# Hybrid attention/DeltaNet block on one core: half of two blocks' output projection in the lead, inverse sums spread behind a unit's products, no threshold search around block ends

## The chip, the cores and the metric

One NeuronCore of a Trainium2 chip runs the whole program. The metric is the device time of one execution in microseconds (us).

## The reference

One encoder layer over 2048 tokens of width 1024, in float32:

```python
h = rms_norm(x, norm_mix_g);  proj = h @ w_in
o_a = sparse_indexer_attention(...)   # 8 heads of 64, top 256 keys of an indexer's score
o_b = gated_deltanet(...)             # 4 heads of 128, chunks of 64
x = x + concatenate([o_a, o_b]) @ w_out
h = rms_norm(x, norm_ffn_g)
x = x + square(relu(h @ w_ff1)) @ w_ff2      # width 4096
return rms_norm(x, norm_final_g)
```

What matters here is the line with `w_out`. Its 1024 input rows are 512 rows of attention output and 512 rows of DeltaNet output. The DeltaNet half of all tokens is known before attention starts.

## The kernel before

The program has three phases. The first normalises and projects, the second runs the DeltaNet, the indexer's scores and the rest of the projection, and the third (`attention_and_mlp`) runs attention, the output projection and the MLP. Only the third is touched.

**Blocks, tiles, units.** The third phase treats 16 tiles of 128 tokens in 4 blocks of 512. Attention is done in 64 units `u` (two heads of a tile, four units a tile). A unit is: scores (L2210, L2211) into PSUM, mask and maximum on VectorE (L2040, L2047), exponential on ScalarE (L1932), transposes (L2225), a high part on ScalarE (L1921) and a low part on VectorE (L2060), products with the values (L2243), the lower half copied on ScalarE (`low`, L1927), and `finish` on VectorE (L2020, L2024), which multiplies by the inverse sums. The inverse sums (reciprocal, L2067) are spread over the partitions by two small transposes, `spread` (L2252). Queries and keys are rotated and split beforehand by `prep` items, three for each tile (`sin` L1799, `add` L1806 and `prep_low` L1812 on GpSimd, `cos` L2073 on VectorE).

**Dense work.** Every float32 product is three fp32r matmuls (`three`, L2140 to L2142: high by high, high by low, low by high). For each block the dense stream is O (output projection, 8 chains of 24 matmuls), then W1 and W2. Weights come in units of 128x1024, are loaded by SyncE (`weights`, L1694), rounded on ScalarE (L1905) and have their low part made on GpSimd (`split`, L1784). A block uses 72 units, 288 in all. A dense step is half a unit: 12 matmuls of 512 columns. Its input, the mix, is split into `ah` and `al` by `mix_high` (ScalarE, L1898) and `mix_low` (VectorE, L2013), eight pieces a block: four are loaded (`mix_in`, L1760) from the DeltaNet's result through two buffers, four are the attention's rows. `x_add` (L1962) adds a chain of O to the residual; squares, their sum (L1969, PE L2191), `root`, `norm` (L1993) and `h_high` (L1888) follow.

**Threshold search.** For tiles 8 to 15 the 256th largest score is found bit by bit: `probe` on ScalarE (L1841 counts over up to 2048 columns, L1843 and L1847 set the bit), 31 probes a tile, and 11 `select` steps on VectorE (begin, turn, fix and so on). That makes 8 times 42 = 336 steps, one behind another.

**Order.** `OverlapPlan` writes all this into numbered slots. In each slot every engine's steps stand in the order of `ORDER`, and every engine runs its own list strictly in order, with semaphore waits. Slots below 0 are the lead: block 0's attention (units 0 to 15, three slots each, `LEAD` 58 slots before slot 0) with no dense work. From slot 0 a block has 147 slots: 144 dense steps and 3 without, while the next block's units are spread over it (`begins`). Search steps run from slot 2 to 377. `weights` for unit n stands one slot behind the split of unit n-2, and the splits of weight units 0 and 1 stand five slots behind the first. `search`, `mlp` and `attention` of the plan fill the lists; `number` counts banks.

```python
if i == 0:
    self.put("pe", end, "spread", u)      # ORDER has spread before product
self.put("pe", end, "product", u, i)
...
s = self.unit_slot[n - 2] if n >= 2 else self.first + 5
self.put("pool", s, "split", n)
...
if u: pe.wait_ge(norm_done, u)            # in spread: the bank shared with product is free
pe.wait_ge(rinv_done, u + 1)
```

## Time and profile before

| | |
|---|---|
| median of 3 runs | 3702.31 us (3700.27 to 3706.99) |
| profiled execution | 3707.24 us, span 3705.4 us, mean granted TensorE clock 0.959 |
| third phase | from about 1414 us; first dense step at 1539.3 us |
| busy | PE 3309.7 (89%), PEld 2733.7 (74%), DVE 2159.5 (58%), ACT 2160.7 (58%), POOL 1347.2 (36%) |
| chain that ended last | PE 28%, ACT 16%, DVE 9%, issue 5%, POOL 2%, DMA 1% |
| DMA | 395.42 MB, mean 107 GB/s |

The span is what the hardware profiler saw from the first to the last instruction. PE is the matmul, PEld the weight load beside it. The granted clock of TensorE is given as a share of 2.4 GHz, so 0.5 is 1.2 GHz. Since matmuls are pipelined, a PE that is shown busy all the time may still run below its full pace; the number of matmuls in a stretch and PEld tell that.

### The profile page before, as it was taken

What the parts mean: (1) busy time and instruction counts of PE and PEld (TensorE: products, weight loads), DVE (VectorE), ACT (ScalarE), POOL (GpSimd) and SP (SyncE); (2) the same over time, 40 slices, a digit from 0 to 9 for tenths busy, and PEclk for the clock granted to TensorE, in tenths of its full rate; (3) what the DMA queues carried; (4) which work ended last, traced back from release to release, by engine and by line L of the source; (5) the groups of instructions that cost most, each with busy time, mean ns of one, the idle gap of its engine ahead of it and who ended that gap; (6) DMA issues with size and microseconds to landing.
All of it is one profiled execution on the core that took longest, in us unless ns stands there. A gap on an engine that the chain in (4) does not pass through costs nothing.

```text
span 3705.4 us, 47047 instructions
## 1 busy us (share of the span) xinstructions
PE 3309.7 (89%) x16674; PEld 2733.7 (74%) x16674; DVE 2159.5 (58%) x3704; ACT 2160.7 (58%) x3717; POOL 1347.2 (36%) x713
## 2 busy tenths in 40 slices
PE   6999878888899995789899889999889999989998
PEld 4888757777777773668787668788668878868886
DVE  6344038687977764646646675748676575443223
ACT  4222138577755653587696869696868944433232
POOL 0211053434345444334444333433323333334443
PEclk9999989999999996899999999999999999999999
DMA  3512253423433444323333433334333333332222
GB/s 118 238 57 85 88 122 74 126 65 74 118 97 80 102 130 117 105 77 125 109 103 119 135 105 104 113 107 129 117 110 119 102 110 97 97 128 91 97 97 80
DMA packets 282664, 395.42 MB, mean 107 GB/s; under 512 B 22832, under 2 KB 204208, under 8 KB 277808
## 3 DMA queue, kind: packets, MB, share of 16 engines
q1 hardware_dynamic: 277680, 360.97, 32.0%
q10 hardware_dynamic: 4752, 31.46, 2.3%
q8 instruction: 134, 2.20, 0.2%
q14 instruction: 98, 0.80, 0.1%
HBM read 320.61 MB, written 71.73 MB: 106 GB/s over the span
## 4 chain that ended last, share of the span: by engine, by line
PE 28%; ACT 16%; DVE 9%; issue 5%; POOL 2%; DMA 1%; SPq 0%; ACTq 0%; DVEq 0%; POOLq 0%
PE m_ps L2140 7%; PE m_ps L2142 7%; PE m_ps L2141 7%; ACT m_junk L1841 6%; ACT m_wh L1905 2%; PE m_ps L2243 2%; POOL m_wl L1784 2%; PE m_ps L2225 2%; ACT m_prob L1932 1%; ACT m_verdict L1843 1%; ACT m_trial L1847 1%; ACT m_phi L1921 1%; PE m_ps L2210 1%; PE m_ps L2211 1%; DVE m_rl L1980 1%
## 5 line engine op out<-in xcount | busy, mean ns | idle before, releaser
L1784 POOL TENSOR_TENSOR m_wl<-m_raw,m_wh 128x1024 fp32r<-128x1024 f32 x288 | 719.0, 2497 | 1327.6 <-ACT m_wh L1905 1327.6
L2140 PE MATMUL m_ps<-m_ah,m_wh 128*128 128x512 f32 x1280 | 523.4, 409 | 25.1 <-DVE m_al L1997 17.3
L2142 PE MATMUL m_ps<-m_ah,m_wl 128*128 128x512 f32 x1280 | 507.0, 396 | 0.0
L2141 PE MATMUL m_ps<-m_al,m_wh 128*128 128x512 f32 x1280 | 505.8, 395 | 0.0
L2140 PE MATMUL m_ps<-m_th,m_wh 128*128 128x512 f32 x1024 | 414.9, 405 | 17.9 <-DVE m_tl L1982 11.3
L2142 PE MATMUL m_ps<-m_th,m_wl 128*128 128x512 f32 x1024 | 404.5, 395 | 0.0
L1841 ACT ACTIVATE m_junk<-m_sc,m_trial 128x1152 int8<-128x1152 f32 (+7 forms) x248 | 401.5, 1619 | 4.4 <-DVE m_sc L2100 3.3
L2141 PE MATMUL m_ps<-m_tl,m_wh 128*128 128x512 f32 x1024 | 403.6, 394 | 0.0
L1905 ACT ACTIVATE m_wh<-m_raw 128x1024 fp32r<-128x1024 f32 x288 | 302.9, 1052 | 146.8 <-PE m_ps L2142 138.9
L1980 DVE TENSOR_TENSOR m_rl<-m_rl 128x512 f32<-128x512 f32 x128 | 104.5, 816 | 358.5 <-ACT m_th L1861 358.1
L2140 PEld LDWEIGHTS m_ps<-m_ah,m_wh 128*128 128x128 f32 x1280 | 244.7, 191 | 79.9 <-DVE m_al L1997 20.1
L1921 ACT ACTIVATE m_phi<-m_ps 128x512 fp32r<-128x512 f32 (+1 forms) x288 | 164.2, 571 | 227.7 <-PE m_ps L2225 223.3
L2060 DVE TENSOR_TENSOR m_plo<-m_ps,m_phi 128x512 fp32r<-128x512 f32 (+1 forms) x288 | 189.4, 658 | 176.2 <-ACT m_phi L1921 174.9
L1975 DVE TENSOR_TENSOR m_acc<-m_acc,m_ps 128x512 f32<-128x512 f32 x256 | 175.0, 684 | 190.5 <-PE m_ps L2142 188.7
L2142 PEld LDWEIGHTS m_ps<-m_ah,m_wl 128*128 128x128 f32 x1280 | 244.0, 191 | 53.5
L1228 DVE SCALAR_TENSOR_TENSOR i_score<-i_relu,i_w,i_score 128x512 f32<-128x512 f32 (+3 forms) x266 | 255.1, 966 | 48.0 <-ACT i_relu L1086 33.6
L2141 PEld LDWEIGHTS m_ps<-m_al,m_wh 128*128 128x128 f32 x1280 | 245.1, 191 | 44.2 <-issue 0.5
L1086 ACT ACTIVATE i_relu<-i_ps 128x512 f32<-128x512 f32 (+3 forms) x304 | 156.0, 546 | 171.8 <-PE i_ps L884 135.0
L2140 PEld LDWEIGHTS m_ps<-m_th,m_wh 128*128 128x128 f32 x1024 | 195.1, 191 | 58.2 <-DVE m_tl L1982 13.0
L2142 PEld LDWEIGHTS m_ps<-m_th,m_wl 128*128 128x128 f32 x1024 | 194.6, 190 | 42.6
L2040 DVE CUSTOM_DVE_ANT_0 m_prob<-m_ps,m_bias 128x512 f32<-128x512 f32 (+3 forms) x320 | 192.2, 606 | 57.2 <-PE m_ps L2211 55.7
L2141 PEld LDWEIGHTS m_ps<-m_tl,m_wh 128*128 128x128 f32 x1024 | 195.4, 191 | 36.1
(324 smaller groups left out, 7470.3 us busy)
## 6 DMA issues: line engine op xcount, KB each, us to landing
m_raw<-w_units SPq DMA_DIRECT2D x288, 512.0 KB, 3.3
m_vals<-valsT SPq DMA_DIRECT2D x240, 128.0 KB, 3.4
p_raw<-w_proj SPq DMA_DIRECT2D x72, 256.0 KB, 4.1
m_rot<-rowsQ SPq DMA_DIRECT2D x50, 256.0 KB, 4.4
projT<-work ACTq DMA_DIRECT2D x12, 1024.0 KB, 4.5
g_qkvz<-projT SPq DMA_DIRECT2D x16, 768.0 KB, 5.5
wraw<-w_proj SPq DMA_DIRECT2D x21, 512.0 KB, 5.0
i_rot<-projT SPq DMA_DIRECT2D x32, 256.0 KB, 5.0
```

The lines of the kernel that those rows point to most:

```text
L1086: nc.scalar.activation(relu[:, c % RELUS, 0:w], ips[:, c % 2, 0:w], ACT.Relu).then_inc(relu_done, 1)
L1228: nc.vector.scalar_tensor_tensor(out=to, in0=relu[:, c % RELUS, 0:w], scalar=w_idx[:, j, h:h + 1], in1=to, op0=ALU.mult, op1=ALU.add).then ...
L1784: nc.gpsimd.tensor_tensor(wl[:, n % 3, :], raw[:, n % 2, :], wh[:, n % 3, :].bitcast(fp32), ALU.subtract).then_inc(w_lo, 1)
L1841: turns.do(nc.scalar.activation(junk[:, 0:N], sc[:, 0:N], ACT.Sign, scale=-1.0, bias=trial[:, :].bitcast(fp32), accum_out=balance[:, :]))
L1905: nc.scalar.activation(wh[:, n % 3, :], raw[:, n % 2, :], ACT.Copy).then_inc(w_hi, 1)
L1921: nc.scalar.activation(p_hi[:, m % 2, 0:w], t_bank(r)[:, 0:w], ACT.Copy).then_inc(hi_done, 1)
L1975: nc.vector.tensor_tensor(acc[:, k, :], acc[:, k, :], f_bank("W2", b, g, k), ALU.add).then_inc(y_added, 1)
L2040: nc.vector.tensor_tensor_reduce(out=prob[:, u % 2, h, 512 * p:512 * p + w], in0=s_bank(n)[:, 0:w], in1=bias[:, 512 * p:512 * p + w], scal ...
L2060: nc.vector.tensor_tensor(p_lo[:, m % 2, 0:w], t_bank(r)[:, 0:w], p_hi[:, m % 2, 0:w].bitcast(fp32), ALU.subtract).then_inc(lo_done, 1)
L2140: nc.tensor.matmul(dst, hi, rh, start=first, stop=False)
L2141: nc.tensor.matmul(dst, hi, r_low, start=False, stop=False)
L2142: return nc.tensor.matmul(dst, lo, rh, start=False, stop=last)
```

## The change

Weights of w_out are laid out for blocks 0 and 1 (`AHEAD` = 2) in halves: 4 "lead" units with the DeltaNet half of two output chunks each, shared by both blocks, and 4 "OA" units a block with the attention half. In the lead 16 dense steps of 12 matmuls (block 0 or 1, output chunk k) compute the DeltaNet half; step m stands five slots behind the begin of unit m, that is between the transposes of unit m+1 and its products. `lead_add` on VectorE adds each to x rows, loaded in 8 transfers of 512 KB (`lead_in`), stored in 8 transfers (`lead_out`) to a DRAM tensor `addedT`, from which `x_in` of blocks 0 and 1 then loads in place of x. The four DeltaNet pieces of the mix of blocks 0 and 1 are loaded early and whole (`gdn_in`) into memory that the search and the probabilities use later, and are split early in the lead. Blocks 0 and 1 lose the first half of each O chain: 139 slots, and 142 with three empty ones added behind block 1's second step. The splits of the first two weight units move to 14 and 16 slots behind the first. The search starts at slot -9 and ends at 364, and leaves out the ten slots from eight before to one behind the begin of blocks 1 and 2. `spread` moves to the last turn of a unit, behind `product`; `product` takes over the wait for the bank, and `finish` waits for `spread`. Tables get two buffers.

```diff
-        "pe": "spread product scores values transpose dense squares".split(),
+        "pe": "product spread scores values transpose dense squares".split(),
...
+        short = [x for x in dense if x[0] != "O" or x[2]]
+        gap = [("gap", 0, 0)]
+        self.dense = [short, short[:2] + 3 * gap + short[2:]] + [dense] * (self.NB - self.AHEAD)
...
+        self.lead = [(b, 2 * j + y) for j in range(KC // 2) for b in range(self.AHEAD) for y in range(2)]
+        self.lead_slot = [self.begins(n) + 5 for n in range(len(self.lead))]
...
+    def split_slot(self, n):
+        return self.unit_slot[n - 2] if n >= 2 else self.first + 14 + 2 * n
...
-            self.put("sp", self.first if t < 1 else prep_at[3 * t - 1] + 1, "table_in", t)
+            self.put("sp", self.first + t if t < 2 else prep_at[3 * t - 4] + 1, "table_in", t)
...
-                if i == 0:
+                if i == self.turns(t) - 1:
                     self.put("pe", end, "spread", u)
...
+        ends = {x for b in range(1, self.NB) for x in range(self.base[b] - KC, self.base[b] + 2)}
+        free = [x for x in range(-12, stop + 1) if x not in ends]
...
-            span = (stop - 2) * weight(j) / total
+            span = (len(free) - 5) * weight(j) / total
...
-            self.put("sp", self.first + 2 if n < 2 else self.first + 3 if n < 4 else self.unit_slot[n - 4] + 1, "weights", n)
-            s = self.unit_slot[n - 2] if n >= 2 else self.first + 5
+            self.put("sp", self.first + 3 + 5 * n if n < 2 else self.split_slot(n - 2) + 2, "weights", n)
+            self.put("act", self.split_slot(n), "split", n)
+            self.put("pool", self.split_slot(n) + (n < 2), "split", n)
+        for m, (b, k) in enumerate(self.lead):
+            s = self.lead_slot[m]
+            self.put("pe", s, "dense", b, "lead", k, 0)
+            self.put("dve", s + 1, "lead_add", b, k)
...
+                if i < MIX_LOADED and b < self.AHEAD:
+                    s = self.first + 14 + 3 * b + i // 2
...
+            def lead_add(b, k):
+                c = plan.chain_of[b, "lead", k, 0]
+                n, row = c // 2, lead_rows[:, c // 2 % HOMES, c % 2, :]
+                dve.wait_ge(lead_in[n % HOMES], 16 * (n // HOMES + 1))
+                dve.wait_ge(chain_done, c + 1)
+                nc.vector.tensor_tensor(row, row, f_bank("lead", b, k, 0), ALU.add).then_inc(lead_added, 1)
...
+                if u and i == 0:
+                    pe.wait_ge(norm_done, u)
                 o = ps[:, O_BANK, 0:2 * P]
```

## Rows read from the trace of the kernel before

**Rows 1.** Busy by stage: window, length, then busy us and count of each engine, clock, DMA share, GB/s
```profile
1410.00:1442.00 32.00, 2.81 (x10) 2.18 (x11) 4.85 (x12) 5.56 (x10) 14.08 (x15) 0.54 0.63 181
1442.00:1525.00 83.00, 52.71 (x249) 42.94 (x249) 59.30 (x199) 42.69 (x117) 37.28 (x34) 0.70 0.34 97
1525.00:1539.30 14.30, 4.83 (x20) 3.76 (x19) 6.11 (x15) 5.19 (x10) 2.55 (x2) 0.51 0.38 111
1539.30:1607.60 68.30, 59.22 (x272) 47.48 (x270) 36.91 (x72) 53.65 (x105) 25.41 (x13) 0.92 0.31 98
```

**Rows 2.** Longest of PE's waits in the lead, 1410 to 1540 us: total, times, longest
```profile
PE m_ps L2252 <- DVE m_mixed L2024: 23.3, 15, 3.0
```

**Rows 3.** Timeline of the lead's start: start, us, engine, line, operation, idle before
```profile
1422.62 0.69 DVE L2073 TENSOR_TENSOR m_acc<-m_acc,m_table 128x512 f32<-128x512 f32 x1 [2.04 <-DMA m_acc<-rowsQ]
1422.97 12.25 SPq L1694 DMA_DIRECT2D m_raw<-w_units  x4
...
1430.23 4.64 POOL L1784 TENSOR_TENSOR m_wl<-m_raw,m_wh 128x1024 fp32r<-128x1024 f32 x2 [8.78 <-ACT m_wh L1905]
...
1434.83 1.25 POOL L1799 TENSOR_TENSOR m_acc<-m_acc,m_table 128x512 f32<-128x512 f32 x1
...
1439.48 0.48 PE L2210 MATMUL m_ps<-m_keys,m_qhi 128*128 128x128 f32 x1 [19.19 <-POOL m_qlo L1812]
```

**Rows 4.** Timeline, PE: one stretch of block 3, dense work alone
```profile
3399.80 0.39 PE L2140 MATMUL m_ps<-m_ah,m_wh 128*128 128x512 f32 x1
...
3401.16 0.39 PE L2140 MATMUL m_ps<-m_ah,m_wh 128*128 128x512 f32 x1
```

**Rows 5.** Timeline, PE: the first dense step of block 0
```profile
1539.90 0.63 PE L2141 MATMUL m_ps<-m_al,m_wh 128*128 128x512 f32 x1
1540.33 0.63 PE L2142 MATMUL m_ps<-m_ah,m_wl 128*128 128x512 f32 x1
```

**Rows 6.** PE's wait at the lead's end, 1525 to 1539.3 us
```profile
PE m_ps L2225 <- ACT m_prob L1932: 9.0, 1, 9.0
```

**Rows 7.** Timeline, ACT: one probe of the search, and what follows
```profile
1558.34 1.24 ACT L1841 ACTIVATE m_junk<-m_sc,m_trial 128x1152 int8<-128x1152 f32 x1
...
1560.37 0.83 ACT L1932 ACTIVATE m_prob<-m_prob,m_nmx 128x640 f32<-128x640 f32 x1
```

**Rows 8.** Windows around the begins of blocks 1, 2 and 3, columns as in rows 1
```profile
2045.00:2078.10 33.10, 26.34 (x107) 20.90 (x106) 18.50 (x30) 29.64 (x53) 10.09 (x4) 0.90 0.30 100
2078.10:2118.60 40.50, 33.42 (x153) 26.02 (x152) 27.50 (x46) 35.27 (x60) 13.57 (x7) 0.92 0.58 178
2118.60:2160.30 41.70, 36.14 (x172) 28.04 (x171) 30.25 (x55) 27.76 (x49) 14.21 (x7) 0.92 0.32 101
...
3242.30:3266.60 24.30, 22.32 (x98) 17.87 (x97) 16.98 (x21) 10.90 (x18) 7.18 (x3) 1.00 0.36 119
3266.60:3305.30 38.70, 28.74 (x102) 21.43 (x102) 18.79 (x20) 10.64 (x15) 12.37 (x5) 0.82 0.49 163
```

**Rows 9.** Waits of PE around the begin of block 1, 2045 to 2160.3 us
```profile
PE m_ps L2140 <- DVE m_tl L1982: 5.3, 1, 5.3
```

**Rows 10.** Windows between begins: blocks 0 and 2 with probes, block 3, columns as rows 1
```profile
1847.40:1901.30 53.90, 53.90 (x268) 45.25 (x267) 26.35 (x59) 50.36 (x89) 23.68 (x11) 1.00 0.31 101
...
2849.10:2917.40 68.30, 64.23 (x332) 53.82 (x330) 37.93 (x80) 61.73 (x95) 23.42 (x11) 0.98 0.31 100
...
3470.00:3490.00 20.00, 20.00 (x90) 16.55 (x89) 4.14 (x6) 5.67 (x8) 9.35 (x4) 1.00 0.23 80
```

**Rows 11.** Waits of PE, 1539 to 3000 us: the wait of the spread for the inverse sums
```profile
PE m_ps L2252 <- DVE m_rinv L2067: 14.4, 10, 4.0
```

**Rows 12.** Groups at the lead's end: line, shapes, count, busy us, mean ns, idle before
```profile
L2013 DVE TENSOR_TENSOR m_al<-m_tmp,m_ah 128x512 fp32r<-128x512 f32 x4 | 2.8, 692 | 5.9 <-ACT m_ah L1898 5.8
L1898 ACT ACTIVATE m_ah<-m_tmp 128x512 fp32r<-128x512 f32 x4 | 2.5, 629 | 7.0 <-DMA m_tmp<-mixT 7.0
```

**Rows 13.** The page: the high part of a weight unit
```profile
L1905 ACT ACTIVATE m_wh<-m_raw 128x1024 fp32r<-128x1024 f32 x288 | 302.9, 1052 | 146.8 <-PE m_ps L2142 138.9
```

More of the change, by code:

```diff
@@ L1386 @@
     ORDER = {
-        "sp": "weights values_in values_out values_back table_in prep_in bias_in score_in x_in mix_in out bias_out".split(),
+        "sp": "values_in values_out values_back table_in prep_in weights bias_in score_in x_in mix_in out bias_out gdn_in lead_in lead_out".split(),
         "pool": "split bias_set sin add prep_low".split(),
         "act": "relu square low values_hi high split exp round mix_high h_high probe root".split(),
-        "dve": "x_add y_add sum_squares ff_low finish mask values_low lower rinv cos prep_low mix_low norm out select".split(),
-        "pe": "spread product scores values transpose dense squares".split(),
+        "dve": "x_add y_add sum_squares ff_low finish mask values_low lower rinv cos prep_low mix_low norm out lead_add select".split(),
+        "pe": "product spread scores values transpose dense squares".split(),
     }
     LEAD, SHORT, SPARE, GAP = 58, 3, 8, 3
+    AHEAD, HOMES = 2, 4
     def __init__(self, S, topk):
@@ L1406, in __init__ @@
         self.stream = stream
-        self.dense = []
+        self.units = [("lead", j, 0) for j in range(KC // 2)] + [("OA", j, 0) for j in range(KC // 2)] + stream
+        dense = []
         for kind, a, b in stream:
-            self.dense += [(kind, a, 2 * b), (kind, a, 2 * b + 1)]
+            dense += [(kind, a, 2 * b), (kind, a, 2 * b + 1)]
             if (kind, a) == ("O", KC - 1):
-                self.dense += [("O end", 0, 0)] + [("gap", 0, 0)] * (self.GAP - 1)
-        i = self.dense.index(("W1", 0, 1))
@@ L1413, in __init__ @@
-        self.dense[i], self.dense[i + 1] = self.dense[i + 1], self.dense[i]
-        self.FB = len(self.dense)
-        self.first = self.begins(-4) - 2
-        self.unit_slot = [b * self.FB + self.dense.index((kind, x, 2 * y)) for b in range(self.NB) for kind, x, y in stream]
+                dense += [("O end", 0, 0)] + [("gap", 0, 0)] * (self.GAP - 1)
+        i = dense.index(("W1", 0, 1))
+        dense[i], dense[i + 1] = dense[i + 1], dense[i]
+        short = [x for x in dense if x[0] != "O" or x[2]]
@@ new lines, in __init__ @@
+        gap = [("gap", 0, 0)]
+        self.dense = [short, short[:2] + 3 * gap + short[2:]] + [dense] * (self.NB - self.AHEAD)
+        self.base = [sum(len(x) for x in self.dense[:b]) for b in range(self.NB + 1)]
+        self.first = self.begins(-4) - 2
+        self.lead = [(b, 2 * j + y) for j in range(KC // 2) for b in range(self.AHEAD) for y in range(2)]
+        self.lead_slot = [self.begins(n) + 5 for n in range(len(self.lead))]
+        self.weights = [(-1, "lead", j, 0) for j in range(KC // 2)]
@@ new lines, in __init__ @@
+        for b in range(self.NB):
+            for kind, x, y in self.units[KC // 2:KC] + stream[KC:] if b < self.AHEAD else stream:
+                self.weights.append((b, kind, x, y))
+        self.unit_of = {x: n for n, x in enumerate(self.weights)}
+        self.unit_slot = [self.lead_slot[2 * self.AHEAD * x] if kind == "lead" else
+                          self.base[b] + self.dense[b].index(("O", 2 * x, 1) if kind == "OA" else (kind, x, 2 * y))
+                          for b, kind, x, y in self.weights]
@@ L1546, in mlp @@
                 self.put("dve", s, "mix_low", b, i)
-                self.put("sp", self.prep_end + 1 if b == 0 else base + 2 + i // 2, "x_in", b, i)
-            for i, (kind, x, half) in enumerate(self.dense):
+                self.put("sp", max(self.prep_end + 1, x_free) if b == 0 else base + 2 + i // 2, "x_in", b, i)
+            for i, (kind, x, half) in enumerate(self.dense[b]):
                 s = base + i
@@ L1592, in number @@
         self.ring_at = {x: n for n, x in enumerate(self.ring)}
-        begins = [x for x in pe if x[0] == "dense" and (x[2] == "W2" or x[4] == 0) or x[0] == "squares" and x[3] == 0]
-        self.bank_turns = [("norm", x[1], x[2]) if x[0] == "squares" else (x[2], x[1], x[3], x[4]) for x in begins]
+        begins = [x for x in pe if x[0] == "dense" and (x[2] == "W2" or x[4] == self.opens(x[1], x[2])) or x[0] == "squares" and x[3] == 0]
+        self.bank_turns = [("norm", x[1], x[2]) if x[0] == "squares" else (x[2], x[1], x[3], x[4] if x[2] == "W2" else 0) for x in begins]
         self.bank_turn = {x: n for n, x in enumerate(self.bank_turns)}
@@ L1773, in _ @@
                     does[what](*x)
-            for k in range(KC):
-                sp.wait_ge(o_stored[k], 16 * NB)
+            for k in range(2):
+                sp.wait_ge(o_stored[k], 16 * KC // 2 * NB)
         @block.gpsimd
```

217 lines of the change are left out of this document (133 added, 84 removed).

## The prediction

> **What bounds the kernel now.** I read the windows by stage first, then the waits, then the timeline where a wait was long. The third phase has two regimes. In the lead nothing is saturated: between 1442 and 1525 us PE is busy 52.7 of 83 us at a mean granted clock of 0.70, VectorE 59.3, ScalarE 42.7 [rows 1]. What limits it is the loop of a unit through PE, ScalarE and VectorE in order; its mark is PE's wait for the unit before to be finished, 23.3 us over 15 units [rows 2]. From 1539.3 us on the dense stream is the backbone. In block 3, with no attention beside it, the start-to-start time is (3401.16 - 3399.80) / 6 = 0.227 us, a dense step of 12 is 2.72 us [rows 4]. While probes of the search run, ScalarE is as full as PE: 50.4 of 53.9 us in one stretch of block 0, 61.7 of 68.3 in block 2 [rows 10]. Around the begins of blocks neither is: the last sums, the norm and the next mix follow one another.
>
> **What leaves the blocks, block 0.** Its first 19 slots take 68.3 us, ScalarE busy 53.7 of them [rows 1]. Eight dense steps go, 8 x 2.72 = 21.8 us of PE, with 8 slots. All that attention and search do in them stays; four splits of a weight unit, 1.05 us of ScalarE each [rows 13], go too. If PE set the pace, 27 us would go (eight slots of the average 68.3/19 = 3.6 us come to 29); if ScalarE did, only these 4 us. The search now runs all through this stretch: a probe costs 1560.37 - 1558.34 = 2.03 us of ScalarE [rows 7], and with spans 17/164 of 352 steps of room there are 1.25 a slot. For 11 slots that is 28 us, with squares, splits and attention some 47 us. **I take -21**, between -4 and -29.
>
> **Block 1.** The 27 slots from eight before its begin to its first W1 take 33.1 + 40.5 + 41.7 = 115.3 us, for about 24 dense steps of 2.72 us plus attention [rows 8]. Here 8 steps go (21.8 us), 8 slots go and 3 empty ones come, the mix's four loaded pieces need no ScalarE, VectorE or transfer (4 x (0.63 + 0.69) = 5 us [rows 12]), and ten slots have no probe. What the probes cost there can be bounded by block 3's begin, which has none: its eight slots before take 24.3 us where block 1's take 33.1, 9 us less, part of it because no attention stands there; but the eight after take 38.7 against 40.5, so that gap is the norm's own chain [rows 8]. The 5.3 us wait for `m_tl` is a probe in front of a relu [rows 9], and a probe may still stand in the slot just ahead of the cleared ones. **I take -32** (21.8 of PE, 5 from cleared slots, 5 from the mix), between -12 and -45. Block 2's begin keeps all its work and only loses probes: **-5**, between -9 and 0.
>
> **The search squeezed.** 336 steps stood in 375 slots, now in 352 usable ones, of which about 11 lie in the lead. By slots 11 (after) and 19 (before), the same place in the work, some 7 more probes are done. But the cleared and the missing slots put about 13 more steps into the 304 slots between the begins, 13 x 2.4 = 31 us of an engine (the estimate of 2.4 is the probe of rows 7 with its count grown to wider tiles). How much of that shows depends on who paces. Block 0's stretch has PE busy all 53.9 us, block 2's 64.2 of 68.3 [rows 10], so by matmul busy almost nothing should show. The weight loads say it differently: block 3, in full flow, has 16.55/20 = 83%, block 0 has 45.25/53.9 = 84%, block 2 has 53.82/68.3 = 79%. So in block 0 PE paces, in block 2 ScalarE costs it some 5%. **I take +20**, between 0 and +31. The Trainium skill, Perfetto Trace Analysis, section on identifying the most-contended engine, says that matmul busy is no good measure of how near TensorE is to its limit and that the share of weight loads is. By matmul busy the term would be near 0 and the forecast 20 us lower; by weight loads it stands, and the trace's counts agree with the page.
>
> **The lead's start.** The first query cannot be scored until 1439.5 us [rows 3]. Its rotation on VectorE runs at 1422.6, but GpSimd's half only at 1434.8: in front of it in GpSimd's list stand the splits of weight units 0 and 1, which wait for a transfer and ScalarE until 1430.2 and take 4.64 us. SyncE is blocked for 12.25 us as well, because loads 2 and 3 wait for these splits. After the change the splits stand nine and eleven slots later, so GpSimd can go on at 1422.7: up to 12.1 us earlier. Against it ScalarE's list soon holds a split and mix pieces that wait for 1 MB of `gdn_in` and a 0.5 MB weight unit, and the mix's 16 pieces of 0.63 and 0.69 us [rows 12] all lie in the first slots. **-9**, between -12 and +3.
>
> **The lead's middle.** 16 dense steps come in: 16 x 2.72 = 43.6 us at the full clock. Each stands between the transposes of a unit and its products, just where PE waits now, and 30.3 us of the 83 are idle [rows 1, 2]. `lead_add` (about 0.69 us, as a VectorE piece of this shape in rows 12) comes 16 times on VectorE, 11 us where 23.7 are idle; it stands behind its chain and ahead of the next mask, which waits for PE anyway. GpSimd gets four splits more of 4.64/2 = 2.3 us [rows 3], 9 us where 45.7 are idle, but one stands ahead of a `prep_low`. Below nothing, because existing work at 0.70 of the clock would run faster, to all 44 us: the bounds are -8 and +44. I take **+8**, nearer the hidden side, since the measured idle time per unit (1.9 us) and the faster clock together nearly make 2.72. The clock: the first dense matmuls of block 0 start 1540.33 - 1539.90 = 0.43 us apart [rows 5], the half clock's pace, yet the stretch they open has 0.92 on average against 0.51 before it [rows 1]: dense work brings 2.4 GHz back soon.
>
> **The lead's end.** 14.3 us lie between the last products and the first dense step, PE waits 9.0 us and ScalarE 7.0, the latter for the loaded mix [rows 1, 6, 12]. These loads go: -7. But the search's begin and about 8 probes now stand ahead of the last mix pieces in ScalarE's list: 8 x 2.03 = 16 [rows 7]. **+9**, between -7 and +14.
>
> **Spread behind product.** In the lead the bank's wait only changes its owner, from spread to product: 0, the finish before still has to end. In the blocks spread waits 14.4 us in 10 places for the inverse sums [rows 11]; that goes, and part comes back as product's wait for the high part. **-6**, between -14 and 0. `finish` waits for a spread that PE runs right behind the product: nothing, while `low` on ScalarE lies in between. Two table buffers, and 16 transfers of 512 KB more in the lead against a DMA share of 0.34 [rows 1]: SyncE is in order, and its new waits (`lead_out` for `lead_add`, `weights` for a split) stand ahead of later `prep_in`: **+2**, between -4 and +8.
>
> **Sum.** -21 - 32 - 5 + 20 - 9 + 8 + 9 - 6 + 2 = -34 us on the profiled 3707.2 us, that is 3673; the median of the runs is 4.9 us lower, so 3668.
>
> **Rivals.** (1) *The lead does not hide it, and the clock stays low.* At 1.2 GHz a step is 12 x 0.43 = 5.1 us [rows 5], 16 of them 82 us; with 30 us of idle time filled, +52 in place of +8. That is 3668 + 44 = 3712, slower. It decides if the lead's clock stays near 0.70. For it: 0.54 and 0.70 in the lead, and three engines in a tight loop. Against it: the rise from 0.51 to 0.92 when dense work begins [rows 1]. Chance 0.20. The Trainium skill, TensorE: Matmul & The Clock Gate, section "What's actually happening", says that the default is throttled and activity releases it; by that rule this rival falls to the 44 us of the full clock less what is hidden, and rows 1 and 5 agree. (2) *ScalarE paces the blocks.* Then the dense steps removed were not on the path: block 0 gives 8 in place of 21, block 1 gives 15 in place of 32: 3668 + 30 = 3698, no change. For it: ScalarE 93% in the blocks. Chance 0.15. (3) *The lead is free and the clock rises.* The middle is -8, the search squeezed +8: 3668 - 28 = 3640. Chance 0.20. The forecast itself has 0.45.
>
> **Numbers.** 0.2% is 7.4 us, about what a measurement of this kernel can tell from no change. Faster: 0.45 + 0.20 and a third of rival 2, 0.70. Same 0.10, slower 0.20. The range goes from rival 3 with a little of the terms' lower bounds, 3630, to beyond rival 1, 3720.
>
> **What would show it.** Right: first query scores near 1430 us; 16 dense steps in the lead at a clock near 0.9 with a few us more between spreads; block 0's first W1 step some 10 us earlier than 1607.6; the begin of block 1 some 30 us shorter, that of block 2 about 5; the stretches between somewhat longer, ScalarE full. Wrong: a first O step of block 0 later than 1560 us, or a clock near 0.7 in the lead (rival 1); block 0 and 1 begins that shrink by less than 15 us each (rival 2).

## The result and the profile after

| | before | after |
|---|---|---|
| median, 4 runs each | 3704.65 us (3700.27 to 3708.22) | 3736.03 us (3730.64 to 3739.48) |
| ratio to before, 95% | | 1.008 (1.0066 to 1.0094) |
| profiled execution, span | 3707.24, 3705.4 | 3735.05, 3733.2 |

The change costs 31 us, where 34 us less were forecast. The page of after: the totals, then the chain that ended last.

```profile
span 3733.2 us, 47221 instructions
PE 3322.6 (89%) x16674; PEld 2742.3 (73%) x16674; DVE 2164.2 (58%) x3720; ACT 2157.0 (58%) x3713; POOL 1344.9 (36%) x709
...
PE 28%; ACT 16%; DVE 10%; issue 5%; POOL 2%; DMA 1%; SPq 0%; DVEq 0%; ACTq 0%; POOLq 0%
```

The same number of matmuls, ScalarE as busy as before to 4 us, nearly the same chain. No total tells where 28 us of span went. So I cut both traces at the same places of the work: the first scores, the second half of block 0's second O chain, the first W1 step and the last W2 group of each block. Lengths between these places, in us, worked out from the start times in the two timelines:

```
stretch                          before   after   after - before
up to the first scores           1439.5  1427.2   -12.3
lead, and first O steps           111.4   127.5   +16.1
rest of O and norm, block 0        56.7    38.2   -18.5
between begins, block 0           437.4   466.5   +29.1
begin of block 1                  115.3    95.3   -20.0
between begins, block 1           461.7   492.9   +31.2
begin of block 2                  119.7   112.6    -7.1
between begins, block 2           500.6   512.3   +11.7
rest                              463.1   460.8    -2.3
```

In what follows "begin" and "between begins" are these stretches, and "head" is what lies between block 0's first O step and its first W1 step. Of the 58 us forecast for block 0's head and the two begins, 45.6 came; block 1's begin, at 20.0 of 32, is furthest off. Between the begins, where I had allowed 20 us in all, 72 were lost.

Two cautions on the first lines. The phases ahead of the third end at slightly different times in different executions, though no edit here touches them: the first transpose of the values starts at 1419.8 us in before, at 1418.0 in after, and between 1414.7 and 1424.5 over all the profiled runs. From it to the first scores it is 19.6 us in before and 9.2 in after, so 10.4 of the 12.3 us belong to the change. And the second stretch holds three half O steps in before but only one in after. From the first scores to block 0's first O step, where no O step counts, the lead grew from 99.8 to 116.1 us.

First the lead. Windows of after; columns are window, length, then busy us (and count) of PE, PEld, DVE, ACT, POOL, then clock, DMA share, GB/s.

```profile
1410.00:1444.80 34.80, 5.85 (x22) 4.49 (x22) 16.68 (x28) 11.31 (x24) 20.03 (x19) 0.50 0.89 246
1444.80:1543.30 98.50, 81.38 (x448) 68.40 (x446) 75.17 (x225) 58.16 (x141) 43.82 (x35) 0.93 0.64 192
1543.30:1592.90 49.60, 37.47 (x143) 27.80 (x143) 24.52 (x48) 46.84 (x95) 14.41 (x8) 0.76 0.21 63
```

Against [rows 1] the granted clock of the lead's middle is 0.93 in place of 0.70, with 448 matmuls where 249 stood. Over the same places of the work, from the first scores to block 0's first O step, it is 0.67 in before and 0.87 in after:

```profile
1439.50:1539.30 99.80, 59.89 (x274) 48.67 (x275) 66.94 (x220) 48.83 (x131) 42.25 (x37) 0.67 0.35 99
```

```profile
1427.20:1543.30 116.10, 86.77 (x466) 72.69 (x466) 87.58 (x248) 66.99 (x161) 57.43 (x43) 0.87 0.70 210
```

PE's longest waits in it, after (total, times, longest), and the first query's scores:

```profile
PE m_ps L2305 <- DMA m_vraw<-projT: 11.5, 1, 11.5
PE m_ps L2314 <- ACT m_prob L2008: 11.2, 2, 9.9
PE m_ps L2299 <- POOL m_qlo L1889: 9.5, 2, 8.8
PE m_ps L2334 <- DVE m_plo L2145: 7.8, 2, 6.9
```

```profile
1427.19 0.47 PE L2299 MATMUL m_ps<-m_keys,m_qhi 128*128 128x128 f32 x1 [8.78 <-POOL m_qlo L1889]
```

The first of these waits stands ahead of all scores and is in before too (11.4 us). The 23.3 us in 15 places of [rows 2] are gone: the dense steps fill them. The scores start 12.3 us earlier than in [rows 3]. What stands in place of [rows 6] is a wait of 9.9 us for an exponential on ScalarE, which now has five probes in a row in front of it, from 1530.84 us on:

```profile
1538.99 1.25 ACT L1918 ACTIVATE m_junk<-m_sc,m_trial 128x1152 int8<-128x1152 f32 x1
...
1541.03 0.83 ACT L2008 ACTIVATE m_prob<-m_prob,m_nmx 128x640 f32<-128x640 f32 x1
```

```profile
1542.09 1.09 PE L2314 MATMUL m_ps<-m_ident,m_prob 128*128 128x128 f32 x4 [9.89 <-ACT m_prob L2008]
```

Then between the begins, before and after:

```profile
1607.60:2045.00 437.40, 411.78 (x1942) 336.33 (x1943) 248.61 (x453) 342.10 (x613) 183.55 (x87) 0.98 0.33 107
...
2045.00:2160.30 115.30, 95.90 (x426) 74.95 (x425) 76.24 (x130) 92.67 (x162) 37.87 (x18) 0.91 0.41 128
2160.30:2622.00 461.70, 442.03 (x2215) 367.04 (x2216) 305.71 (x554) 363.36 (x581) 180.02 (x87) 0.99 0.35 112
```

```profile
1592.90:2059.40 466.50, 427.24 (x1972) 349.75 (x1973) 254.00 (x467) 363.24 (x652) 183.60 (x87) 0.95 0.34 103
2059.40:2154.70 95.30, 73.62 (x306) 56.17 (x304) 59.29 (x114) 56.62 (x96) 27.23 (x14) 0.84 0.38 118
2154.70:2647.50 492.80, 453.20 (x2240) 374.63 (x2241) 313.09 (x569) 382.50 (x613) 186.08 (x87) 0.98 0.35 107
```

In block 0's stretch ScalarE has 39 instructions and 21.1 us more, PE only 30 matmuls more. The begin of block 1 has 36 us of ScalarE less, but it is only 20 shorter. Work has moved out of the begins into the stretches between them.

### The profile page after: what moved, and what is told of

It is laid out like the page before. It is cut to its first block, busy times and chain, and to the rows that moved or that the text cites. A ratio compares the mean times of both kernels' runs of the same rounds, so it can differ in the third digit from the quotient of the medians.

```text
span 3733.2 us, 47221 instructions
## 1 busy us (share of the span) xinstructions
PE 3322.6 (89%) x16674; PEld 2742.3 (73%) x16674; DVE 2164.2 (58%) x3720; ACT 2157.0 (58%) x3713; POOL 1344.9 (36%) x709
## 4 chain that ended last, share of the span: by engine, by line
PE 28%; ACT 16%; DVE 10%; issue 5%; POOL 2%; DMA 1%; SPq 0%; DVEq 0%; ACTq 0%; POOLq 0%
PE m_ps L2225 7%; PE m_ps L2227 7%; PE m_ps L2226 7%; ACT m_junk L1918 7%; ACT m_wh L1981 2%; PE m_ps L2334 2%; PE m_ps L2314 2%; ACT m_prob L2008 1%; ACT m_verdict L1920 1%; POOL m_wl L1861 1%; ACT m_trial L1924 1%; DVE m_rl L2063 1%; ACT m_phi L1997 1%; DMA out_dram<-m_tmp 1%; PE m_ps L2299 1%
## 5 line engine op out<-in xcount | busy, mean ns | idle before, releaser
L1861 POOL TENSOR_TENSOR m_wl<-m_raw,m_wh 128x1024 fp32r<-128x1024 f32 x284 | 706.0, 2486 | 1368.7 <-ACT m_wh L1981 1368.7
L2225 PE MATMUL m_ps<-m_ah,m_wh 128*128 128x512 f32 x1280 | 533.3, 417 | 37.9 <-DVE m_al L2080 23.2
```

What stands on the lines that cost most here:

```text
L1861: nc.gpsimd.tensor_tensor(wl[:, n % 3, :], raw[:, n % 2, :], wh[:, n % 3, :].bitcast(fp32), ALU.subtract).then_inc(w_lo, 1)
L2225: nc.tensor.matmul(dst, hi, rh, start=first, stop=False)
```

## The experiments

My theory after the result was that the slots without search cost more than they give: between begins ScalarE is as full as PE, so a search step put there is paid in full, while at a begin it rode along. The rivals: the dense steps taken out of the blocks' heads were never on the path, and attention, which now falls on fewer slots, lengthens the stretches; the search in the lead holds up the first O step; the moved spread costs; the later loads cost. Each was undone in after or made alone in before. All diffs are to before or after as named, and lines left out of them are marked by three dots.

**1. Search allowed around the ends of blocks, in after (a_ends).**

```diff
-        ends = {x for b in range(1, self.NB) for x in range(self.base[b] - KC, self.base[b] + 2)}
+        ends = set()
```

> The kernel after, with search steps allowed again around the ends of blocks (the search still starts in the lead): 20 slots more, so 336 steps in 372 slots in place of 352. Theory A, the squeezed search: in the kernel after the stretches between the block ends grew by 29, 31 and 12 us where their engine ScalarE gets some 5% more search steps a slot; with the room given back most of that returns, 3736 - 30 to 50 = 3690 to 3705 us, the block ends growing by 10 to 20 us at the same time. Theory B, the moved inverse sums or something else in the attention units is what lengthened those stretches: under 8 us change, 3728 or more, with the stretches as long as after. Theory C, the exclusion helps as meant: slower than 3736.

Measured: 3701.37 us (3694.95 to 3709.93), ratio to before 0.9992 (0.9983 to 1.0002). That is 35 us less than after: one line of the change carries its whole loss. The stretches between begins fall to 449.7 and 477.4 us. The begin of block 1 grows by 6.1 us only, less than the 10 to 20 expected.

**2. The same line alone, in before (b_ends).**

```diff
+        ends = {x for b in range(1, self.NB) for x in range(b * self.FB - KC, b * self.FB + 2)}
+        free = [x for x in range(stop + 1) if x not in ends]
...
-                slot = int(at + 1 + i * (span - 3) / len(steps))
+                slot = free[int(at + 1 + i * (span - 3) / len(steps))]
```

> The kernel before, with nothing but the search steps kept out of the ten slots around each block's begin (336 steps in 355 slots in place of 375). Theory A: slower by 15 to 40 us, with ScalarE's probes 5% denser between the begins, which grow by more than the begins shrink. Theory B: within 8 us of before, the begins some 5 us shorter each and nothing else longer. Theory C: faster by about 10 us.

Measured: 3745.55 us (3742.61 to 3746.41), ratio 1.0107 (1.0093 to 1.012), 40 us slower than before. Windows of b_ends, from the first W1 step of block 0:

```profile
1612.50:2061.80 449.30, 416.15 (x1942) 340.01 (x1943) 246.29 (x451) 354.22 (x637) 186.09 (x86) 0.97 0.34 104
2061.80:2176.30 114.50, 96.18 (x427) 74.40 (x425) 76.24 (x130) 79.10 (x134) 37.91 (x18) 0.90 0.42 129
2176.30:2654.60 478.30, 446.21 (x2215) 369.45 (x2216) 306.74 (x557) 374.90 (x602) 185.32 (x87) 0.98 0.35 109
```

Compare them with the windows of before above. The begin of block 1 gives up 13.6 us of ScalarE and gets 0.8 us shorter; block 2's gets 0.9 shorter. Block 0's stretch gets 12.1 us more of ScalarE and 11.9 us longer. The stretch of block 1 grows by 16.6, that of block 2 by 7. Counted in the traces, 11 probes have left the two begins, 10 of them for the stretches between and one for block 0's head. The search steps of those 20 slots had cost next to nothing where they stood, and cost 40 us, some 3.6 us a probe, where they went.

**3. Half of the probes (b_half, a_half, as_half).** These leave out the lower 16 of the 31 probes of a tile, so the threshold is found only to the upper half of its bits; as_half is after with the search as in a_start (experiment 5), so it also has search steps around the ends of blocks.

```diff
+                if bit < 16:
+                    return
                 if bit == BITS - 1:
...
-                dve.wait_ge(probed, (3 * BITS + 3) * (n + 1))
+                dve.wait_ge(probed, 47 * (n + 1))
```

> The kernel before with the lower 16 of the 31 probes of each search left out (the threshold is found to the upper half of its bits only): 128 probes of some 2.0 to 2.8 us each, about 310 us, leave ScalarE. Theory A (ScalarE paces while probes run): clearly faster, by 50 to 120 us, since PE then paces. Theory B (PE paces everywhere but at the begins): by less than 20 us. This run is the base of the next.

> The kernel after with the same 16 probes of each search left out. Theory A: with ScalarE relieved the moved projection shows its gain, so this is FASTER than the kernel before with the same probes left out, by 20 to 50 us (the lead about equal, the begins of blocks 0 and 1 shorter, the stretches between equal). Theory B, the lead or the moved inverse sums cost the time: it stays 20 to 35 us SLOWER than its base, as the full kernels do.

> The kernel after with search steps allowed around block ends, the search started at slot 2, and the lower 16 probes of each search left out. Against 3647 for the kernel before with the same probes out. If ScalarE's probes alone eat the gain of the moved projection: 3647 - 35 to 50 = 3597 to 3612. If the squeezed attention costs without probes as well: 3620 to 3635.

Measured: b_half 3647.1 us (3644.38 to 3650.82), ratio 0.9843 (0.983 to 0.9856); a_half 3640.8 (3633.83 to 3643.33), 0.9822 (0.9809 to 0.9836); as_half 3630.64 (3625.94 to 3635.36), 0.9799 (0.9786 to 0.9813). With half the probes after is faster than before by 6 us, not slower by 31: 38 us hang on the probes. But 6 us are far from the 20 to 50 that I had expected. With the search out of the lead and allowed around the ends as well, the gain is 16.5 us, inside the range that I had given for attention that costs without probes too. Block 0's stretch of b_half, then that of as_half:

```profile
1604.20:2010.60 406.40, 399.96 (x1941) 332.96 (x1942) 247.28 (x455) 248.03 (x418) 187.31 (x87) 1.00 0.37 115
```

```profile
1570.00:1991.90 421.90, 408.53 (x1973) 339.90 (x1974) 252.77 (x466) 260.88 (x451) 185.33 (x87) 0.98 0.37 114
```

Even so the stretch is 15.5 us longer with the new plan, though ScalarE is busy for 62% of it. So part of what the stretches lose is not the search's; counted in the traces, one attention unit more is finished in it (14 against 13), and PE is idle for 13.4 us in place of 6.4.

**4. The spread behind the product, alone in before (b_spread), and put back in a_ends (ae_spread).**

```diff
-        "pe": "spread product scores values transpose dense squares".split(),
+        "pe": "product spread scores values transpose dense squares".split(),
...
-                if i == 0:
+                if i == self.turns(t) - 1:
                     self.put("pe", end, "spread", u)
...
+                    last = nc.tensor.transpose(...)
+                last.then_inc(spread_done, 1)
```

> The kernel before with only the spread of the inverse sums moved behind a unit's last product (product takes over the wait for the bank, finish waits for spread). The stretches between the block begins stay 12 and 16 us longer than before even with the search's room given back. Theory D, the moved spread lengthens them: 10 to 25 us slower than before. Theory E, it is the denser attention in shorter blocks: within 7 us of before, or up to 8 faster as forecast (PE's 14.4 us wait for the inverse sums gone).

> The kernel after with search steps allowed around block ends, and the spread put back ahead of a unit's first product. Theory D: faster than that kernel without this edit (3701) by 10 to 25 us, 3676 to 3691. Theory E: 3698 to 3710.

Measured: b_spread 3710.14 us (3699.3 to 3716.77), ratio 1.0009 (1.0 to 1.0018), 3 us slower than its before, at the edge of what can be told. ae_spread 3696.92 us (3688.05 to 3701.58), ratio 0.9974 (0.9965 to 0.9983), 4.5 us below a_ends; by the ratios, since the two did not run on the same occasion, 0.0018 or 7 us. PE's waits of b_spread, 1539 to 3000 us:

```profile
PE m_ps L2246 <- DVE m_plo L2061: 30.5, 25, 4.3
...
PE m_ps L2246 <- ACT m_phi L1921: 10.9, 10, 2.4
```

The wait of [rows 11], 14.4 us, is gone. In before these two waits were 22.9 us in 20 places and 7.5 in 8: 11 of the 14 us come back at once as waits for the two parts of the probabilities. By the places of the work nothing is gained between begins (437.9 and 462.4 us in b_spread, 437.4 and 461.7 in before); the begin of block 1 is 2.5 us shorter, and the lead, from the first scores to the first O step, is 5.1 us longer (104.9 against 99.8). So the loss lies in the lead. Why the lead grows isn't settled.

**5. Where the search begins, in a_ends: at slot 2 as in before (a_start), or 24 slots earlier still (a_early).**

```diff
-        free = [x for x in range(-12, stop + 1) if x not in ends]
+        free = list(range(0, stop + 1))       # a_start
+        free = list(range(-36, stop + 1))     # a_early
```

> The kernel after with search steps allowed around block ends, and the search started at slot 2 as before, not at slot -9. 336 steps in 360 slots in place of 372. If room for the search is worth what the ten-slot exclusions showed (35 us for 20 slots, 1.7 us a slot), this is 3701 + 15 to 20 = 3716 to 3721 in sum, with the lead's end some 10 us shorter and the blocks 25 to 30 us longer. If the search in the lead costs what it gives: 3701 within 7 us.

> The kernel after with search steps allowed around block ends, and the search started 24 slots earlier, at slot -33, inside the lead: 336 steps in 396 slots. If a slot of room is worth 1.7 us: the blocks 30 to 40 us shorter, the lead longer by what of some 24 steps of 2 us is not hidden there (10 to 30 us), in sum 3680 to 3700. If the lead is as tight as the blocks: 3700 to 3715.

Measured: a_start 3691.97 us (3685.98 to 3698.24), ratio 0.9967 (0.9956 to 0.9978), 9 below a_ends. a_early 3716.5 (3712.63 to 3719.6), 1.0029 (1.0019 to 1.004), 15 above. Both miss what was expected: a_start was to be slower or the same, and a_early to be 3715 at most. The lead up to the second half of the second O chain takes 108.8 us in a_start, 125.4 in a_ends and 156.1 in a_early, 111.4 in before. The lead's windows, a_start and then a_early:

```profile
1432.40:1541.20 108.80, 89.25 (x480) 75.19 (x481) 87.84 (x248) 59.62 (x145) 58.11 (x44) 0.90 0.69 207
```

```profile
1432.00:1588.10 156.10, 104.83 (x480) 84.27 (x481) 99.50 (x264) 118.27 (x272) 61.19 (x45) 0.78 0.52 160
```

The 16 dense steps (480 matmuls against 325 in before's 111.4 us) are all but free. The fair comparison leaves out the O steps at the end and takes a kernel with the later splits but without the dense steps, which is b_split of experiment 9. From the first scores to block 0's first O step, b_split and then a_start:

```profile
1423.80:1528.70 104.90, 58.53 (x274) 47.66 (x275) 67.40 (x220) 50.84 (x133) 46.94 (x39) 0.66 0.42 117
```

```profile
1432.40:1538.30 105.90, 86.35 (x467) 72.78 (x467) 84.94 (x241) 57.41 (x142) 57.52 (x43) 0.90 0.68 205
```

192 matmuls more cost 1 us. Search in the lead is not free. In after, with 9.6 us more of ScalarE than a_start between these places, they are 10.3 us further apart. Against a_start, a_early has 58.7 us more on ScalarE up to the second half of the second O chain and a lead 47.3 longer, and the clock falls back to 0.78. In a_ends 16.6 us are paid in the lead for 7.5 saved in block 0's stretch (449.7 against 457.2).

**6. Search from slot 2, all slots, spread as before (as_spread).** This is the change's projection in the lead with the exclusion, the search's early start and the moved spread taken back. The later splits, the order of loads and the second table buffer stay in.

> The kernel after with search steps allowed around block ends, the search started at slot 2, and the spread back ahead of the first product. Summing the single edits (search start -9 us, spread -4 us from 3701): 3688, some 18 us under before. If the two share one cause: 3692.

Measured: 3688.59 us (3686.99 to 3693.2), ratio 0.996 (0.9946 to 0.9973). It beats both kernels: 17 us below before, 47 below after. Its windows, from the second half of the second O chain:

```profile
1536.70:1572.90 36.20, 29.09 (x133) 22.10 (x131) 25.12 (x49) 25.23 (x48) 13.99 (x8) 0.91 0.42 139
1572.90:2024.20 451.30, 414.75 (x1970) 340.31 (x1971) 252.67 (x466) 355.84 (x646) 184.24 (x87) 0.98 0.34 106
2024.20:2119.80 95.60, 73.51 (x306) 55.96 (x304) 57.67 (x105) 88.02 (x155) 27.67 (x14) 0.84 0.38 117
2119.80:2602.40 482.60, 451.37 (x2240) 373.50 (x2241) 320.87 (x574) 365.23 (x587) 180.28 (x87) 0.98 0.35 109
```

The rest of O in block 0 is 20.5 us shorter than in before and the begin of block 1 19.7; but the stretches behind them are 13.9 and 20.9 longer. Over the third phase, from the first transpose of the values on, the profiled execution is 19.8 us shorter than that of before. Step by step, 10.5 us less to the first scores; 5.4 more to the first O step; 29.0 less in block 0's head, 13.9 more behind it; 19.7 less at block 1's begin, 20.9 more behind it; the rest 0.8 less. The first two terms come from the later splits: b_split has them too (experiment 9).

**7. The opposite of the excluded slots: ten slots around the begins of blocks 1 and 2 count twice for the search (b_dup in before, as_dup in as_spread).**

```diff
+        ends = {x for b in range(1, self.NB) for x in range(b * self.FB - KC, b * self.FB + 2)}
+        free = sorted([*range(stop + 1), *(x for x in ends if x <= stop)])
...
-                slot = int(at + 1 + i * (span - 3) / len(steps))
+                slot = free[int(at + 1 + i * (span - 3) / len(steps))]
```

> The kernel before with the opposite of the exclusion: the ten slots around the begins of blocks 1 and 2 count twice for the search, so steps are 5% thinner between them. Keeping steps out of them cost 40 us. If ScalarE's density between the begins is all that counts, this is 15 to 40 us faster than before, 3667 to 3692, with longer begins. If the begins have only so much idle time, the gain is used up there: 3697 to 3710.

> As as_spread, with the slots around the begins counted twice for the search as in b_dup. As there: 15 to 35 us under as_spread (3655 to 3675) if density between the begins is all, 3680 to 3695 if the begins are used up.

Measured: b_dup 3728.38 us (3721.42 to 3732.75), ratio 1.0062 (1.0049 to 1.0074), 23 slower than before. as_dup 3698.47 (3691.32 to 3704.3), 0.9981 (0.9972 to 0.9989), 10 above as_spread. Both are above every range that I had given. Windows of b_dup:

```profile
1606.30:2037.50 431.20, 408.97 (x1944) 336.57 (x1943) 250.51 (x455) 330.58 (x593) 185.28 (x87) 0.98 0.35 109
2037.50:2172.40 134.90, 98.48 (x426) 75.12 (x425) 80.30 (x129) 107.13 (x188) 36.28 (x18) 0.89 0.36 109
```

14.5 us more of ScalarE at the begin of block 1 cost 19.6 us, and the stretch, relieved of 11.5 us, gives back 6.2. Block 1's stretch, relieved of 9.6 us, gives back only 0.5. A slot at a begin carries its one search step for nothing and no second one. In as_dup, whose plan is denser, the two stretches do give back what they are relieved of (9.0 us for 9.6, 10.7 for 12.3), but the begin of block 1 takes 14.0 us for 14.0.

**8. Dense steps taken out, their slots kept (as_gap).** In as_spread, blocks 0 and 1 keep 147 slots: where a half O step went, an empty slot stands.

```diff
-        short = [x for x in dense if x[0] != "O" or x[2]]
+        short = [x if x[0] != "O" or x[2] else ("gap", 0, 0) for x in dense]
...
-        self.dense = [short, short[:2] + 3 * gap + short[2:]] + [dense] * (self.NB - self.AHEAD)
+        self.dense = [short, short] + [dense] * (self.NB - self.AHEAD)
```

> As as_spread (3689), but blocks 0 and 1 keep 147 slots: the first half of each O chain is an empty slot in place of none, so attention and search are as thin as in the kernel before. Theory F, squeezed attention: the stretches between the begins come back to 437 and 462 us within 5 us, the block begins give back a part (5 to 12 us each), in sum 3675 to 3690. Theory G, something else: the stretches stay at 451 and 483.

Measured: 3716.0 us (3712.27 to 3727.51), ratio 1.0028 (1.0015 to 1.0041), 10 slower than before. Neither theory held whole: block 0's stretch came back to within 4 us of before, block 1's stayed 17 longer, and the sum is 26 us above theory F's range. Windows of as_gap:

```profile
1540.80:1596.00 55.20, 37.96 (x149) 28.05 (x147) 23.75 (x60) 47.01 (x96) 10.95 (x6) 0.79 0.27 86
1596.00:2037.40 441.40, 412.22 (x1943) 339.31 (x1942) 249.97 (x453) 344.08 (x617) 184.60 (x86) 0.97 0.34 107
2037.40:2150.90 113.50, 78.98 (x330) 59.50 (x329) 70.18 (x127) 85.01 (x151) 28.64 (x14) 0.85 0.33 100
2150.90:2629.70 478.80, 448.48 (x2216) 371.37 (x2217) 307.10 (x554) 366.13 (x585) 184.80 (x87) 0.98 0.36 109
```

The rest of O in block 0 takes 55.2 us against 56.7 in before, the begin of block 1 113.5 against 115.3, though they have 72 and 96 matmuls less, at the pace of 0.227 us [rows 4] 16 and 22 us of PE. Taking them out gains 1.5 and 1.8 us. Counted from its first O step, with all eight half steps gone (21.8 us of PE), block 0's head gains 7.0. Most of what shortens the heads in as_spread is the slots that go, since with a slot its search steps and its share of attention go elsewhere.

**9. The order of loads: weights first in SyncE's list and one slot earlier, in as_spread (as_weights); the splits of units 0 and 1, and the loads behind them, later in before (b_split).**

```diff
-            self.put("sp", self.first + 3 + 5 * n if n < 2 else self.split_slot(n - 2) + 2, "weights", n)
+            self.put("sp", self.first + 3 + 5 * n if n < 2 else self.split_slot(n - 2) + 1, "weights", n)
```

That is as_weights, to after, beside `"weights"` moved to the front of the list `"sp"` in `ORDER`; this is b_split, to before:

```diff
-            self.put("sp", self.first + 2 if n < 2 else self.first + 3 if n < 4 else self.unit_slot[n - 4] + 1, "weights", n)
-            s = self.unit_slot[n - 2] if n >= 2 else self.first + 5
+            self.put("sp", self.first + 2 if n < 2 else self.first + 18 if n < 4 else self.unit_slot[n - 4] + 1, "weights", n)
+            s = self.unit_slot[n - 2] if n >= 2 else self.first + 14 + 2 * n
```

> As as_spread, with the loads of weights first in SyncE's slot again and one slot behind a split, not two. Theory F: 3689 within 5 us. Theory G, late weights: 5 to 20 us faster, the stretches between the begins shorter.

> The kernel before with only the splits of weight units 0 and 1 moved from 5 to 14 and 16 slots behind the first, and loads 2 and 3 behind them. The first scores come 10 to 12 us earlier. If the lead is a chain of its own the whole kernel is 8 to 12 us faster (3694 to 3698). If GpSimd's two splits of 2.3 us are then paid further on, 3698 to 3703; if it ends in slots bound otherwise, 3705.

Measured: as_weights 3693.8 us (3686.29 to 3701.06), ratio 0.9964 (0.9952 to 0.9977), not to be told from as_spread. b_split 3700.12 (3693.36 to 3705.34), 0.9978 (0.9969 to 0.9987): its first scores come at 1423.8, 15.7 us earlier than in before, and 6 us are left of it at the end. The traces show where the rest goes: 4.2 of the 15.7 us are phases ahead that ended earlier in this execution, 11.5 are the edit's, and 5.1 of these are paid back in the lead, which takes 105.0 us to the first O step in place of 99.8. Behind it every stretch is as long as in before to 0.4 us.

## Why the prediction was wrong

**The parts.** Undone one after another, by medians of different occasions (the median of before moved between 3704.65 and 3706.81 over them): after 3736.0; search allowed around block ends 3701.4 (-34.7); search out of the lead 3692.0 (-9.4); spread back 3688.6 (-3.4). What is left of the change, the projection in the lead, shorter heads and later splits, is 17 us faster than before; 6 of these the later splits bring alone (b_split). The step for the spread lies within the noise of its two runs; b_spread and ae_spread point the same way. The forecast was right that there is a gain in moving the projection, though it is only 7 to 12 us (as_spread against b_split, by the ratios and by the medians); it was wrong in thinking that the exclusion, the search in the lead and the moved spread would pay for themselves.

**The step that failed is "the search squeezed", +20.** I counted 13 displaced steps, priced them at 31 us if ScalarE were the pace everywhere, then took two thirds and called 31 the upper bound. The count held: between the begins there are 192 probes in before and 204 in after. The price did not. The exclusion alone costs 40 in one kernel and 35 in the other, above the upper bound, so the term was too small even with ScalarE as the pace everywhere: in b_ends the three stretches have 26.5 us more of ScalarE and are 35.7 us longer. Block 0's stretch tells how ScalarE counts there. Its length, ScalarE's busy time and the difference, from windows over the same places of the work:

```
kernel      length   ScalarE   difference
before      437.4    342.1      95.3
b_ends      449.3    354.2      95.1
as_spread   451.3    355.8      95.5
as_gap      441.4    344.1      97.3
a_start     457.2    359.0      98.2
a_ends      449.7    346.6     103.1
after       466.5    363.2     103.3
b_dup       431.2    330.6     100.6
b_half      406.4    248.0     158.4
```

From before to b_ends, and from a_ends to after, where only the search moves, each us more of ScalarE is a us more of the stretch, though ScalarE is busy only 78% of it and PE 94%. (as_spread fits the same line, but as_half is 15.5 us longer than b_half with ScalarE far from full, so there it proves nothing.) Downwards it stops soon: b_dup takes 11.5 us from ScalarE and gets 6.2, b_half takes 94 and gets 31, with PE busy 98% and the clock at 1.00. I read this as a plan that stands at the kink between the two engines. I had read a short window in which PE was busy all the time and concluded from the weight loads, 84% against 83% in block 3, that PE paced block 0 [rows 10]. The whole stretch has 336.33 / 437.4 = 77%, well under block 3's 83%: the row was picked, not typical. The Trainium skill, Perfetto Trace Analysis, section "Identifying the Most-Contended Engine", calls ScalarE's occupancy a fair measure of how near it is to its limit. By that rule 78% leaves room; the measured price of one us for one us says it left none. Of the stretch's other 95 us, 86 are waits of ScalarE's in-order list in before, 72 of them for PE; in b_ends they are 85 and 71, so the added probes filled none of them. The longest in before:

```profile
ACT m_phi L1921 <- PE m_ps L2225: 36.9, 12, 7.3
ACT m_rl L1857 <- PE m_ps L2142: 21.4, 8, 4.1
ACT m_wh L1905 <- PE m_ps L2142: 11.1, 7, 2.2
```

**"-5 from cleared slots", twice.** b_ends gives 0.8 and 0.9. The begin's length is the chain of the last sums, the norm and the next mix, and the search lay beside it. The bound of 9 us came from comparing with block 3's begin [rows 8], and "part of it because no attention stands there" turned out to be nearly all of it. The wait for `m_tl` [rows 9] came as feared: "a probe may still stand in the slot just ahead of the cleared ones". Timeline of after at the end of block 0, ScalarE's probes and the matmul that waits:

```profile
2060.09 1.56 ACT L1918 ACTIVATE m_junk<-m_sc,m_trial 128x1536 int8<-128x1536 f32 x1
...
2062.72 1.56 ACT L1918 ACTIVATE m_junk<-m_sc,m_trial 128x1536 int8<-128x1536 f32 x1
...
2105.95 1.56 ACT L1918 ACTIVATE m_junk<-m_sc,m_trial 128x1536 int8<-128x1536 f32 x1
```

```profile
2067.82 0.79 PE L2225 MATMUL m_ps<-m_th,m_wh 128*128 128x512 f32 x1 [6.11 <-DVE m_tl L2065]
```

No probe starts between 2062.72 and 2105.95 us, but two stand right ahead of the last relu (2065.06 us), and the wait is 6.1 us where it was 5.3.

**Block 0's head -21, block 1's begin -32.** In after the places lost 18.7 and 20.0 us, so read alone the first was right. But in as_spread about half of what the head lost (29.0 us) was pushed on, not saved. From block 0's first O step to its last W2 group as_spread gains 505.7 - 490.5 = 15.2 us, where PE loses eight half steps (21.8 us) and ScalarE's work falls from 395.75 to 383.34. That is nearer ScalarE's 12.4 us than PE's 21.8, and between the -21 of the forecast and the 8 of rival 2. For block 1 nothing is left: 577.0 us in before, 578.2 in as_spread, against the -32 of the forecast and even the 15 of rival 2. So rival 2 had the mechanism about right. Its sign, heads and begins that shrink by less than 15 us each, did not come, because the loss stands behind them. I gave this rival 0.15. The place to see it was [rows 1]: ScalarE busy 53.65 of 68.3 us beside a PE at clock 0.92, which the forecast mentioned and priced at the far bound.

**The lead.** This part held in sum. "First query scores near 1430 us": 1427.2, and the -9 for the lead's start measured -10.4. "16 dense steps at a clock near 0.9": 0.87 from the first scores to the first O step, 0.93 in its middle; so rival 1 is out. Middle and end were put at +8 and +9, and between these two places the lead grew by 16.3. But that is partly luck, since the parts were off: the dense steps cost about 1 us (a_start against b_split), the search 10, and 5 are what the later splits take back, which the forecast had nowhere. In the forecast the end's +9 was to be repaid by a shorter queue later; it was repaid by less than half. "A first O step later than 1560" did not come (first at 1543.3). The clock follows what PE did: from the first scores to the first O step 0.66 and 0.67 without dense work between a lead's units (b_split, before), 0.90 and 0.87 with it (a_start, after), and 0.78 in a_early's lead, where ScalarE holds the dense work up. The Trainium skill, TensorE: Matmul & The Clock Gate, section "What's actually happening", has activity release the throttle, and the traces agree.

**Spread, -6.** Measured +3 and +4.5 (7 by the ratios). The wait did go, but its return was put too low, below the 11 us of 14 that b_spread shows, and the lead, where the forecast had 0, grew by 5.1 in b_spread. With the dense steps in it, it differs by 0.6 only (105.8 us in a_start, 105.2 in as_spread).

**Tables and SyncE, +2.** as_weights shows no cost of the order. The DMA share in the lead rose from 0.34 to 0.64 without a trace in the time.

**What stays open.** In block 1's stretch, as_spread and as_gap are 21 and 17 us longer than before with only 2 to 3 us more of ScalarE; neither the probes (as_half is 20.3 longer than b_half) nor the cut slots (as_gap) account for it, and one attention unit more finished in it (15 against 14; as_gap has 14) does at most for the difference between the two. What as_gap still shares with after, the pieces of the mix loaded early, the residual rows through `addedT`, the second table buffer and `finish` waiting for `spread`, was not undone by itself. Why the exclusion alone costs 16.6 us there for 11.5 of ScalarE isn't settled either.

## What to carry to other kernels

In a schedule of in-order lists with a background task, ask of each slot what the task costs there, not how full the engines are on average: here a step was free at the norm's chain, cost its full time and more between, and a second step in the same slot cost its full time again. To price work moved onto an engine, vary that work alone in both directions and compare the stretch's length with the engine's busy time, since occupancy of 78% hid a price of one for one. Work taken off one of two balanced engines gains little at that place until the other's goes with it (here 1.5, 1.8 or at most 7 us for 16 to 22 us of PE); check this by leaving its slot empty. And compare places of the work, not times from the start: phases that nobody had touched ended up to 10 us apart from run to run.

## What the runs showed of the hardware

The clock of the lead is the one thing of the chip that moved by more than I had put in a sum: 0.66 in b_split to 0.90 in a_start, from the first scores to the first O step, with 16 dense steps of 12 matmuls spread over some 105 us, while the lead got only 1 us longer. Nothing else of the chip was unexpected.
